# A two-layer decoder trunk: one norm of a token pair at a time, tokens loaded first, half of the first modulation sums on TensorE

## The chip, the cores and the metric

One core of a Trainium2 chip. The metric is the device time of one launch in microseconds, over several runs; a profiled execution of the same kernel gives the trace. A difference of 0.2% is about 3 us here.

## The reference

Sequence 512, width 1024, one batch, float32. Two layers: the first has dilated window attention (three groups of heads), the second has differential attention over keys and values that are computed once from the stream after layer 0. Each attention is followed by a gated convolutional feed-forward part. Every part is wrapped as below; the keys and values have a norm and a modulation of their own.

```python
c_act = jax.nn.silu(c)
for l in range(DEPTH):
    shift, scale, gate = ada_mod(c_act, mod_mix_w[l], mod_mix_b[l], 3)   # c_act @ w + b, split in 3
    if l == N_A_LAYERS:
        k_sh, v_sh = shared_kv(x, c_act, kv_norm, kv_mod_w, kv_mod_b, b_w_k, b_w_v, cos, sin)
    h = rms_norm(x, norm_pre_mix[l]) * (1.0 + scale) + shift
    y = mixer(h)                       # dilated (layer 0) or differential attention (layer 1)
    x = x + gate * rms_norm(y, norm_post_mix[l])
    shift, scale, gate = ada_mod(c_act, mod_ffn_w[l], mod_ffn_b[l], 3)
    h = rms_norm(x, norm_pre_ffn[l]) * (1.0 + scale) + shift
    x = x + gate * rms_norm(conv_ffn(h), norm_post_ffn[l])
```

## The kernel before

The program is written engine by engine, each with its own order of instructions, and semaphores between them (`wait_ge(*at.done(signal))`, `.then_inc(*at.here(signal))`). An engine executes its list in order, so a wait holds all that stands behind it. Weights come through a ring of three chunks (`raw`), are split into a high part by ScalarE (`split_head`, L1312) and a low part by VectorE (`split_rest`, L1815), and each product is three matmuls (high x high, high x low, low x high).

**The start.** SP's queue loads six small arrays of vectors (L453 to L456: c and the norm gains, 4 to 8 KB each), then x (L457, 2 MB), then eight tiles of 1 MB of the modulation matrix of layer 0 (`mstart`, L484) with the first value weights among them. ScalarE's queue loads thirteen small things: four lambda vectors, a gain, the positions (L1409 to L1411), and then seven tables of biases and convolution weights (L1412 to L1417). `mstart[:, j]` for j = 0, 1 is the upper and lower half of the rows for shift columns 0 to 511, j = 2, 3 the same for the scale, j = 4 to 7 the same for columns 512 to 1023. The product of c with these tiles is done by VectorE as a chain of multiply-adds (`start_chain`, L2039 and L2041, four instructions for each tile), in the order tiles 0 and 1, 2 and 3, and later 5, then 6 and 7; TensorE takes tile 4 (`shift_columns`, L758). TensorE then sums over the partitions by products with a column of ones (`start_sums`, L606), and VectorE reads the sums (`sums_read`) and makes the gain; only then can the normed and modulated h be made from the turned tokens `z0`, and the first product of TensorE with it begins (`values_chunk`, L777 and L793). Dummy matmuls (`keep_warm`, L578) stand in between. VectorE also computes the rotation angles (L2000 to L2010) before it reads the bias tables (L1976) and starts the chains; the angles go to ScalarE for the sines.

**A token stage** comes after each of the four parts. For four token tiles t: ScalarE sums the squares of y (`square_y`), GpSimd makes the reciprocal root, VectorE adds to x (`gained`, `added`), ScalarE sums the squares of the new x (`square_x`), and TensorE turns x times its root (`turn_x`, L674) into PSUM. Of a pair of tiles, ScalarE writes the front half of the normed columns into a buffer (`fronts`, L1367) and VectorE the back half (`backs`, L1876); ScalarE then makes the high parts (`heads`, L1376) and VectorE the low parts (`rests`, L1890), whose last instruction raises `n_ready`. After layer 0's feed-forward part there are two norms for each pair (`norms` has two entries: one for the shared keys and values, one for layer 1's queries), in the other stages one or none. After that stage TensorE runs `enter_b`: the products of the first value half (L1087) for token tiles 0 and 1, then 2 and 3. `V_BANKS` are the PSUM banks of these four tiles; the first pair is turned into banks 0 to 3, the second into banks 4 to 7.

## Time and profile before

| | |
|---|---|
| median of three runs | 1460.94 us (1459.55 to 1462.33) |
| the profiled execution's own time | 1459.9 us |
| its span, first to last instruction | 1458.0 us |
| TensorE matmul busy | 1407.2 us, 97% |
| VectorE busy | 889.1 us, 61% |
| ScalarE busy | 588.7 us, 40% |
| GpSimd busy | 146.2 us, 10% |
| mean granted TensorE clock | 0.986 |

A row of the timeline gives start, duration, engine, line, operation, output and inputs, count, and in brackets how long the engine had been idle and what ended the wait. PE is TensorE, DVE VectorE, ACT ScalarE, POOL GpSimd; SPq and ACTq are DMA issues. PEclk is the granted clock as a share of 2.4 GHz: 1.00 is 2.4 GHz and 0.50 is 1.2 GHz. A stretch ahead of the first record of the clock is shown as 1.00 whatever it was.

### The profile page before, as it was taken

The page shows a single profiled execution, that of the slowest core. Times are in us where ns is not written, and L with a number is a line of the kernel's source. Part 1 is how long each engine was busy: PE and PEld are TensorE (multiplying, and loading weights), DVE is VectorE, ACT ScalarE, POOL GpSimd, SP SyncE. Part 2 cuts the span into 40 slices and gives each one's busy share as a digit, 9 for nine tenths or more (in the row PEclk, how much of TensorE's full clock was granted, in tenths as well). Part 3 has the DMA queues.
Part 4 walks back from the last instruction along what each step waited for, and adds up shares of the span by engine and source line. Part 5 has one row for each costly group of instructions (what it writes and reads, how often), then busy time and mean ns, then how long its engine had stood idle before and what let it go on. Part 6 is the DMA issues. An engine that isn't in the chain of part 4 may idle for free.

```text
span 1458.0 us, 18234 instructions
## 1 busy us (share of the span) xinstructions
PE 1407.2 (97%) x7091; PEld 1153.7 (79%) x7096; DVE 889.1 (61%) x1572; ACT 588.7 (40%) x1018; POOL 146.2 (10%) x250
## 2 busy tenths in 40 slices
PE   4999999999999999999999999998999999999998
PEld 3789888888798788887887787776888878887886
DVE  7777877674458777763556538887358444443223
ACT  4533444345443334332124526776443333332212
POOL 2001100000211111110112101221221000000000
PEclk9999999999999999999999999998999999999999
DMA  9437423331146655552661221212126333232321
GB/s 334 140 85 233 145 88 117 101 102 30 29 137 199 185 169 178 179 182 87 202 188 58 87 73 58 59 59 87 30 85 186 92 96 92 88 100 89 100 89 70
DMA packets 168667, 171.51 MB, mean 118 GB/s; under 512 B 5269, under 2 KB 140806, under 8 KB 168582
## 3 DMA queue, kind: packets, MB, share of 16 engines
q1 hardware_dynamic: 154224, 119.59, 27.2%
q0 software_dynamic: 13824, 50.34, 10.7%
q8 instruction: 57, 0.93, 0.3%
q10 hardware_dynamic: 534, 0.41, 0.1%
q14 instruction: 28, 0.23, 0.0%
HBM read 168.22 MB, written 2.10 MB: 117 GB/s over the span
## 4 chain that ended last, share of the span: by engine, by line
PE 82%; DVE 8%; ACT 4%; issue 3%; POOL 2%; DMA 1%; SPq 0%; ACTq 0%; DVEq 0%; POOLq 0%
PE ps L624 19%; PE ps L552 15%; PE ps L554 15%; PE ps L553 15%; PE ps L1087 3%; PE ps L900 2%; PE ps L793 2%; PE ps L864 2%; ACT prob L1702 2%; PE ps L606 1%; PE ps L595 1%; PE ps L1204 1%; DVE prob L2355 1%; POOL osum L2537 1%; PE ps L674 1%
## 5 line engine op out<-in xcount | busy, mean ns | idle before, releaser
L552 PE MATMUL ps<-hhi,whi 128*128 128x512 f32 (+1 forms) x1008 | 398.6, 395 | 5.2 <-DVE hlo L1890 4.6
L1815 DVE TENSOR_TENSOR wlo<-raw,whi 128x1024 fp32r<-128x1024 f32 x200 | 244.0, 1221 | 245.7 <-ACT whi L1312 245.4
L554 PE MATMUL ps<-hhi,wlo 128*128 128x512 f32 (+1 forms) x1008 | 390.5, 387 | 0.0
L553 PE MATMUL ps<-hlo,whi 128*128 128x512 f32 (+1 forms) x1008 | 390.1, 387 | 0.0
L1312 ACT ACTIVATE whi<-raw 128x1024 fp32r<-128x1024 f32 x200 | 210.1, 1052 | 257.1 <-PE ps L624 175.7
L552 PEld LDWEIGHTS ps<-hhi,whi 128*128 128x128 f32 x1008 | 191.4, 190 | 47.0 <-issue 6.4
L554 PEld LDWEIGHTS ps<-hhi,wlo 128*128 128x128 f32 x1008 | 191.4, 190 | 41.9
L553 PEld LDWEIGHTS ps<-hlo,whi 128*128 128x128 f32 x1008 | 191.7, 190 | 39.6 <-issue 1.0
L1940 DVE SCALAR_TENSOR_TENSOR macc<-mraw,csil,macc 128x256 f32<-128x256 f32 x294 | 142.2, 484 | 13.4 <-DMA mraw<-in_mod_ffn_w_dram 4.2
L624 PE MATMUL ps<-whi,ghi 128*128 128x512 f32 x352 | 110.8, 396 | 1.7 <-DVE tmp L2294 1.7
L624 PE MATMUL ps<-whi,glo 128*128 128x512 f32 x352 | 110.8, 396 | 0.0
L624 PE MATMUL ps<-wlo,ghi 128*128 128x512 f32 x352 | 110.5, 394 | 0.0
L2278 DVE SCALAR_TENSOR_TENSOR tmp<-ps,convc,tmp 128x511 f32<-128x511 f32 x88 | 65.8, 748 | 51.5 <-ACT tmp L1640 50.0
L1650 ACT ACTIVATE ghi<-tmp 128x512 fp32r<-128x512 f32 x44 | 27.8, 632 | 155.5 <-DVE tmp L2294 155.5
L1640 ACT ACTIVATE tmp<-ps,convc 128x512 f32<-128x512 f32 x44 | 34.2, 778 | 114.6 <-PE ps L554 114.5
L624 PEld LDWEIGHTS ps<-whi,ghi 128*128 128x128 f32 x352 | 65.7, 188 | 18.7 <-DVE tmp L2294 2.6
L624 PEld LDWEIGHTS ps<-wlo,ghi 128*128 128x128 f32 x352 | 66.1, 188 | 16.1
L624 PEld LDWEIGHTS ps<-whi,glo 128*128 128x128 f32 x352 | 66.1, 188 | 15.9
L2500 POOL DMA_DIRECT2D mraw<-in_mod_ffn_w_dram x48 | 36.3, 756 | 352.3 <-DVE macc L1940 279.5
L2294 DVE TENSOR_TENSOR tmp<-ps,tmp 128x512 f32<-128x512 f32 x44 | 30.4, 690 | 58.5 <-issue 45.7
L2472 POOL TENSOR_SCALAR stat<-stat 128x1 f32<-128x1 f32 (+1 forms) x29 | 8.7, 301 | 471.8 <-ACT tmp L1351 426.3
L1647 ACT ACTIVATE tmp<-tmp 128x512 f32<-128x512 f32 x44 | 27.9, 633 | 50.6 <-DVE tmp L2278 50.6
(282 smaller groups left out, 2031.1 us busy)
## 6 DMA issues: line engine op xcount, KB each, us to landing
mraw<-in_mod_ffn_w_dram POOLq DMA_DIRECT2D x48, 512.0 KB, 4.2
raw<-in_ffn_w_gate_dram SPq DMA_DIRECT2D x44, 512.0 KB, 3.8
raw<-in_ffn_w_up_dram SPq DMA_DIRECT2D x44, 512.0 KB, 3.8
raw<-in_ffn_w_down_dram SPq DMA_DIRECT2D x44, 512.0 KB, 3.6
mraw<-in_mod_mix_w_dram POOLq DMA_DIRECT2D x32, 512.0 KB, 3.9
raw<-in_a_w_qkv_dram SPq DMA_DIRECT2D x28, 512.0 KB, 4.1
mstart<-in_mod_mix_w_dram SPq DMA_DIRECT2D x8, 1024.0 KB, 14.5
mraw<-in_kv_mod_w_dram POOLq DMA_DIRECT2D x16, 512.0 KB, 3.8
```

The source lines that it names most:

```text
L552: pe.matmul(out_, whi[:, slot, cols], rhs_hi, start=first, stop=False)
L553: pe.matmul(out_, whi[:, slot, cols], rhs_lo, start=False, stop=False)
L554: return pe.matmul(out_, wlo[:, slot, cols], rhs_hi, start=False, stop=last)
L624: mm = pe.matmul(ps[:, 2 * t + half, :], part[:, k, tile_cols(t)], w[:, half * 512:half * 512 + 512], start=(first and n == 0), stop=(last ...
L1087: mm = pe.matmul(ps[:, V_BANKS[t], :], a[:, k, tile_cols(t)], b[:, slot, w], start=(k == 0 and n == 0), stop=(k == DT - 1 and n == 2))
L1312: act.activation(whi[:, slot, :], raw[:, slot, :], ACT.Copy).then_inc(*at.here(hi_ready, ahead))
L1640: act.activation(tmp[:, 0, :], acc[at.at("bank", 3)], ACT.Identity, bias=convc[:, base + 3 * FT + ft:base + 3 * FT + ft + 1], scale=convc[ ...
L1815: dve.tensor_tensor(wlo[:, slot, :], raw[:, slot, :], head, ALU.subtract).then_inc(*at.here(lo_ready, ahead))
L1940: ins = dve.scalar_tensor_tensor(sum_, src, factor, sum_, ALU.mult, ALU.add)
L2278: ins = dve.scalar_tensor_tensor(conv, bank[:, 0:T - shift], tap(t, ft), conv, ALU.mult, ALU.add)
L2294: dve.tensor_tensor(tmp[:, 2, :], bank, tmp[:, 1, :], ALU.mult).then_inc(*at.here(acc_free))
L2500: pool.dma_start(mraw[:, at.at("mod", 2)], src).then_inc(*at.here(m_landed))
```

## The change

At the start: x is the first load on SP's queue; the six loads of vectors move to the head of ScalarE's queue, ahead of the lambdas and positions; the seven tables are issued after the two exponentials of ScalarE. VectorE reads the tables and runs its chains first, over tiles 0 and 2 (and later 5 and 7) alone; the angles come after them. TensorE multiplies tiles 1, 3, 4 and 6 with c in 16 one-column products each (`start_products`), accumulating in the same bank as the sums: tile 1 ahead of the turning of x, tile 3 between its sixth and seventh column tile, tiles 4 and 6 after the first value chunk. `WARM_SUMS` goes from 12 to 6, in two places. GpSimd makes the root of x ahead of the last mask.

In the stage with two norms: ScalarE and VectorE finish the first norm of a pair before they begin the second, with the splits of weight chunks between them. The second pair is turned into banks 0, 1, 5 and 6, after the value products of two chunks instead of one and after both halves of the second norm's buffer were written; the values of token tiles 0 and 1 go to banks 4 and 7. For one norm the order of instructions stays as it was.

```diff
-    WARM, WARM_START, WARM_SUMS = 24, 8, 12
+    WARM, WARM_START, WARM_SUMS = 24, 8, 6
...
-        V_BANKS = (2, 3, 4, 7)
+        V_BANKS = (4, 7, 2, 3)
+
+        def turned_banks(pair, norms):
+
+            return (0, 1, 5, 6) if pair and norms == 2 else range(4 * pair, 4 * pair + 4)
 
...
 
-            sp.dma_start(rows[C_ROW:C_ROW + DT, 0, :], c[0].rearrange("(r n) -> r n", n=P)).then_inc(*at.here(vec_landed))
-            for dst, src in ((PRE_MIX, norm_pre_mix), (POST_MIX, norm_post_mix), (PRE_FFN, norm_pre_ffn), (POST_FFN, norm_post_ffn)):
-                sp.dma_start(rows[dst:dst + 2 * DT, 0, :], src.rearrange("l (r n) -> (l r) n", n=P)).then_inc(*at.here(vec_landed))
-            sp.dma_start(rows[KVN:KVN + DT, 0, :], kv_norm.rearrange("(r n) -> r n", n=P)).then_inc(*at.here(vec_landed))
             sp.dma_start(x_tok[:], x[0].rearrange("(t p) d -> p t d", p=P)).then_inc(*at.here(x_landed))
...
 
-            def turn_x(t):
-
+            def turn_x(t, norms=1):
+
+                banks = turned_banks(t // 2, norms)
                 pe.wait_ge(*at.done(u_ready, t | 1))
                 pe.wait_ge(*at.done(x_rms, t))
                 for k in range(DT):
...
-                bank = job()
+            def start_columns(half):
+
+                return turned[at.at("tjob", 2)] if half else ps[:, 3, :]
+
+            def start_products(half, j):
+
+                pe.wait_ge(*at.done(c_ready))
                 pe.wait_ge(*at.done(mods_landed[j]))
+                if half and j == 4:
+                    job()
                 for n in range(4):
                     for k in range(DT // 2):
-                        ins = pe.matmul(bank[:, n:n + 1], mstart[:, j, k, tile_cols(n)], csil[:, k:k + 1],
-                                        start=(k == 0), stop=(k == DT // 2 - 1))
+                        row = j % 2 * (DT // 2) + k
+                        pe.matmul(start_columns(half)[:, j // 2 % 2 * 4 + n:j // 2 % 2 * 4 + n + 1], mstart[:, j, k, tile_cols(n)], csil[:, row:row + 1],
+                                  start=(j in (1, 4) and n == 0 and k == 0), stop=False, skip_group_check=True)
+
+            def start_sums(half):
+
+                pe.wait_ge(*at.done(m0_summed, 2 * half + 1))
+                for n in range(8):
+                    ins = pe.matmul(start_columns(half)[:, n:n + 1], macc0[:, n, :], onesf[:, 0:1], start=False, stop=True, skip_group_check=True)
                 job_done(ins)
...
 
+            start_products(0, 1)
             pe.wait_ge(*at.done(x_scaled, 1))
             pe.wait_ge(*at.done(x_scaled_too, 1))
             for k in range(DT):
+                if k == 6:
+                    start_products(0, 3)
                 if k < 4:
                     pe.wait_ge(*at.done(t_free, -1 - k % 2))
                 else:
@@ -816,12 +830,13 @@
                     ins = pe.transpose(ps[:, 4 + k % 4, tile_cols(t)], xn0[:, t, tile_cols(k)], identf[:])
...
             start_sums(0)
-            keep_warm(WARM_SUMS, ps[:, 3, :])
+            keep_warm(WARM_SUMS, ps[:, 2, :])
             values_chunk(0, 0)
-            shift_columns(4)
+            start_products(1, 4)
+            start_products(1, 6)
             values_chunk(0, 1, lambda: start_sums(1))
             keep_warm(WARM_START, ps[:, 4, :])
             values_chunk(0, 2)
@@ -1111,9 +1126,11 @@
                 for c in range(3):
                     pe.wait_ge(*at.done(lo_ready, c))
                     values_b(0, c, (0, 1))
-                    if c == 0:
-                        turn_x(2)
-                        turn_x(3)
+                    if c == 1:
+                        pe.wait_ge(*at.done(full_front, 1))
+                        pe.wait_ge(*at.done(full_back, 1))
+                        turn_x(2, 2)
+                        turn_x(3, 2)
...
-                    for n, norm in enumerate(norms):
-                        fronts(0, norm, n)
+                    fronts(0, norms[0])
                     heads(0, norms[0])
+                    if len(norms) > 1:
+                        split_next()
+                        fronts(0, norms[1])
                     square_x(3)
-                    for norm in norms[1:]:
-                        heads(0, norm)
                     split_next()
-                    split_next()
-                    for n, norm in enumerate(norms):
-                        fronts(1, norm, n)
+                    if len(norms) > 1:
+                        heads(0, norms[1])
+                    else:
+                        split_next()
                     for norm in norms:
+                        fronts(1, norm)
                         heads(1, norm)
...
+            act.dma_start(rows[C_ROW:C_ROW + DT, 0, :], c_rows).then_inc(*at.here(vec_landed))
+            for dst, src in ((PRE_MIX, norm_pre_mix), (POST_MIX, norm_post_mix), (PRE_FFN, norm_pre_ffn), (POST_FFN, norm_post_ffn)):
+                act.dma_start(rows[dst:dst + 2 * DT, 0, :], src.rearrange("l (r n) -> (l r) n", n=P)).then_inc(*at.here(vec_landed))
+            act.dma_start(rows[KVN:KVN + DT, 0, :], kv_norm.rearrange("(r n) -> r n", n=P)).then_inc(*at.here(vec_landed))
             for j, v in enumerate((b_lambda_q1, b_lambda_q2, b_lambda_k1, b_lambda_k2)):
                 act.dma_start(lamr[0:1, j, :], v).then_inc(*at.here(row_landed))
             act.dma_start(row1[0:1, 4, :], b_subln).then_inc(*at.here(row_landed))
             act.dma_start(posi[:], positions.to_broadcast([P, T])).then_inc(*at.here(row_landed))
+
+            act.wait_ge(*at.done(t_free))
+            act.activation(EXPC, vcol[:, C_ROW:C_ROW + DT], ACT.Exp, scale=-1.0).then_inc(*at.here(c_exped))
+            act.wait_ge(*at.done(lam_summed))
+            act.activation(lams[0:1, 2:4], lams[0:1, 0:2], ACT.Exp).then_inc(*at.here(lam_exped))
+            at.passed("tjob", 2)
             act.dma_start(rows[0:6 * DT, 1, :], mod_mix_b.rearrange("l (r n) -> (l r) n", n=P)).then_inc(*at.here(table_landed))
             act.dma_start(rows[6 * DT:12 * DT, 1, :], mod_ffn_b.rearrange("l (r n) -> (l r) n", n=P)).then_inc(*at.here(table_landed))
             act.dma_start(rows[12 * DT:14 * DT, 1, :], kv_mod_b.rearrange("(r n) -> r n", n=P)).then_inc(*at.here(table_landed))
             for layer in range(2):
                 act.dma_start(rows[0:3 * FT, 2 + layer, :], ffn_conv_w[layer].rearrange("w (r n) -> (w r) n", n=P)).then_inc(*at.here(table_landed))
                 act.dma_start(rows[3 * FT:4 * FT, 2 + layer, :], ffn_conv_b[layer].rearrange("(r n) -> r n", n=P)).then_inc(*at.here(table_landed))
-
-
-            act.wait_ge(*at.done(t_free))
-            act.activation(EXPC, vcol[:, C_ROW:C_ROW + DT], ACT.Exp, scale=-1.0).then_inc(*at.here(c_exped))
-            act.wait_ge(*at.done(lam_summed))
-            act.activation(lams[0:1, 2:4], lams[0:1, 0:2], ACT.Exp).then_inc(*at.here(lam_exped))
-            at.passed("tjob", 2)
 
...
-                    for n, norm in enumerate(norms):
-                        backs(0, norm, n)
-                    added(3)
+                    backs(0, norms[0])
+                    if len(norms) > 1:
+                        rests(0, norms[0])
+                        added(3)
+                        split_next()
+                        backs(0, norms[1])
+                        split_next()
+                        rests(0, norms[1])
+                    else:
+                        added(3)
+                        rests(0, norms[0])
+                        split_next()
+                        split_next()
                     for norm in norms:
-                        rests(0, norm)
-                    split_next()
-                    split_next()
-                    for n, norm in enumerate(norms):
-                        backs(1, norm, n)
-                    for norm in norms:
+                        backs(1, norm)
                         rests(1, norm)
...
 
+            bank = job_ready()
+            job_read(dve.tensor_copy(small[:, NEGLAM:NEGLAM + 1], bank[:, 0:1]))
+            for dst, n in ((bcol[:], NMOD), (convc[:, 0:CONV], CONV), (convc[:, CONV:2 * CONV], CONV)):
+                read_columns(dst, n)
+            dve.wait_ge(*at.done(t_free, -1))
+            dve.wait_ge(*at.done(t_free, -2))
...
+            def scale_last_tokens():
+
+                dve.wait_ge(*at.done(x_scale))
+                for t in (2, 3):
+                    dve.tensor_scalar(xn0[:, t, :], x_tok[:, t, :], X_RMS[:, t:t + 1], None, ALU.mult).then_inc(*at.here(x_scaled_too))
+                    at.passed("x_scaled_too")
+
+            def start_chain(j, dst, number):
+
+                sum_ = macc0[:, dst:dst + 4, :].rearrange("p a n -> p (a n)")
+                dve.wait_ge(*at.done(mods_landed[j]))
+                for k in range(DT // 2):
+                    src, row = mstart[:, j, k, :], j % 2 * (DT // 2) + k
+                    if k == 0:
+                        ins = dve.tensor_scalar(sum_, src, csil[:, row:row + 1], None, ALU.mult)
+                    else:
+                        ins = dve.scalar_tensor_tensor(sum_, src, csil[:, row:row + 1], sum_, ALU.mult, ALU.add)
+                    if k < DT // 2 - 1:
+                        chain(ins)
+                ins.then_inc(*at.here(m0_summed, number))
+
+            def sums_read(half):
+
+                bank = job_ready()
+                if not half:
+                    bank = ps[:, 3, :]
+                col, gain = MIX[0] + 4 * half, MIX[0] + DT + 4 * half
+                dve.tensor_tensor(modc[:, col:col + 4], bcol[:, col:col + 4], bank[:, 0:4], ALU.add)
+                job_read(dve.tensor_tensor(modc[:, gain:gain + 4], bank[:, 4:8], bcol[:, gain:gain + 4], ALU.add))
...
+
+            start_chain(0, 0, 0)
+            scale_last_tokens()
+            start_chain(2, 4, 1)
+            dve.wait_ge(*at.done(diffs_ready))
+            diffs = tmp[:, 3, 0:P].bitcast(I32)
+            chain(dve.tensor_single_scalar(diffs, diffs, 3, ALU.bitwise_and))
+            dve.tensor_scalar(near[:, P:2 * P], diffs, 0.0, MASKED, ALU.is_gt, ALU.mult).then_inc(*at.here(near_ready))
+
             a0, a1, k0 = ang[:, 0, :], ang[:, 1, :], ang[:, 2, :]
             two_pi = 2.0 * math.pi
...
-            start_chain((0, 1), 0, 0, scale_last_tokens)
-            start_chain((2, 3), 4, 1)
             split_rest(0)
             sums_read(0)
             h_rest(0, False)
             h_rest(1, True)
             split_rest(1)
-            start_chain((5,), 0, 2)
+            start_chain(5, 0, 2)
             h_rest(2, True)
             h_rest(3, True)
-            start_chain((6, 7), 4, 3)
+            start_chain(7, 4, 3)
             split_rest(2)
-            shift_read()
             sums_read(1)
...
+
+            pool.wait_ge(*at.done(x_squared, NT - 1))
+            rms(X_RMS, X_SUM, slice(0, NT)).then_inc(*at.here(x_scale))
+
+            pool.wait_ge(*at.done(near_ready))
+            select(near[:].rearrange("p (b k) -> p b k", k=P), [[0, 2], [-1, P]], 0, 1, MASKED).then_inc(*at.here(masks_ready))
 
             def token_stage(norms):
                 def of_y(t):
```

## Rows read from the trace of the kernel before

**Rows 1.** Timeline of TensorE, from the start to the first products.

```profile
6.70 2.29 PE L743 MATMUL ps<-onesf,row 1*128 1x1 f32 x10
...
12.97 0.45 PE L735 MATMUL ps<-identf,rows 112*128 112x112 f32 x1 [2.39 <-DMA rows<-in_ffn_conv_b_dram]
...
21.26 5.16 PE L816 MATMUL ps<-identf,xn 128*128 128x128 f32 x32 [3.69 <-ACT xn L1434]
...
31.23 3.54 PE L606 MATMUL ps<-onesf,macc 128*128 128x1 f32 x16 [2.22 <-issue]
...
38.64 0.59 PE L777 MATMUL ps<-whi,hhi 128*128 128x512 f32 x1
...
44.43 3.63 PE L758 MATMUL ps<-csil,mstart 128*128 128x1 f32 x32
...
52.35 1.84 PE L606 MATMUL ps<-onesf,macc 128*128 128x1 f32 x16
```

**Rows 2.** Waits of TensorE from 60 to 370 us: total, times, longest; the first.

```profile
PE ps L614 <- ACT probT L1526: 1.3, 1, 1.3
```

**Rows 3.** Windows of the start: each engine's busy time, PEclk, DMA share, GB/s.

```profile
21.00:24.00 3.00, 2.74 (x13) 2.74 (x14) 2.86 (x5) 1.40 (x3) 0.00 (x0) 1.00 1.05 385
...
31.00:38.00 7.00, 6.77 (x25) 4.63 (x26) 3.37 (x8) 2.73 (x4) 0.29 (x1) 0.51 1.05 387
...
48.00:52.00 4.00, 4.00 (x12) 3.14 (x12) 2.71 (x5) 0.00 (x0) 0.00 (x0) 0.57 0.02 6
```

**Rows 4.** Timeline of the DMA issues of SP and of ScalarE at the start.

```profile
3.38 0.40 SPq L457 DMA_DIRECT2D x_tok<-in_x_dram  x1
...
2.43 0.39 ACTq L1411 DMA_DIRECT2D posi<-in_positions_dram  x1
...
6.22 0.47 ACTq L1417 DMA_DIRECT2D rows<-in_ffn_conv_b_dram  x1
```

**Rows 5.** Timeline of VectorE at the start.

```profile
6.16 0.65 DVE L1972 TENSOR_TENSOR lamr<-lamr 1x128 f32<-1x128 f32 x1 [0.86 <-DMA posi<-in_positions_dram]
...
10.04 0.43 DVE L2000 CAST ang<-posi 128x512 f32<-128x512 int32 x1
...
17.89 0.49 DVE L2039 TENSOR_SCALAR macc<-mstart,csil 128x512 f32<-128x512 f32 x1
...
19.20 1.42 DVE L2028 TENSOR_SCALAR xn<-x_tok,stat 128x1024 f32<-128x1024 f32 x2
...
25.65 5.48 DVE L2041 SCALAR_TENSOR_TENSOR macc<-mstart,csil,macc 128x512 f32<-128x512 f32 x7
...
36.19 0.69 DVE L2075 TENSOR_TENSOR hlo<-tmp,hhi 128x512 fp32r<-128x512 f32 x1 [0.37 <-ACT hhi L1450]
```

**Rows 6.** Timeline of ScalarE at the start.

```profile
8.02 0.21 ACT L1421 ACTIVATE small<-vcol 128x8 f32<-128x8 f32 x1
...
12.50 1.06 ACT L1428 ACTIVATE tmp<-x_tok 128x1024 f32<-128x1024 f32 x1 [4.19 <-DMA x_tok<-in_x_dram]
```

**Rows 7.** Timeline of TensorE around the token stage with two norms.

```profile
794.42 5.13 PE L578 MATMUL ps<-causal,identb 128*128 128x512 bf16 x23
...
802.21 0.57 PE L1087 MATMUL ps<-whi,khi 128*128 128x512 f32 x1 [2.66 <-DVE klo L1890]
...
806.66 3.73 PE L674 MATMUL ps<-macc,x_tok 128*128 128x128 f32 x32
...
817.58 0.50 PE L1087 MATMUL ps<-whi,khi 128*128 128x512 f32 x1 [1.57 <-DVE klo L1890]
```

**Rows 8.** Timeline of ScalarE and VectorE in the same stage, first pair.

```profile
794.68 3.74 ACT L1367 ACTIVATE f_h<-ps,modc,presc 128x256 f32<-128x256 f32 x8
...
799.80 2.35 DVE L1890 TENSOR_TENSOR klo<-f_h,khi 128x1024 fp32r<-128x1024 f32 x2
```

**Rows 9.** Timeline of VectorE in a stage with one norm, second pair.

```profile
410.29 1.90 DVE L1876 TENSOR_SCALAR a_h<-ps,presc,modc 128x256 f32<-128x256 f32 x4 [6.20 <-PE ps L674]
...
413.35 2.36 DVE L1890 TENSOR_TENSOR hlo<-a_h,hhi 128x1024 fp32r<-128x1024 f32 x2 [1.15 <-ACT hhi L1376]
```

84 lines of the change are left out of this document (19 added, 65 removed).

## The prediction

> **What bounds the kernel now.** I read first the timeline of TensorE over the start [rows 1]: the reader is to see that its first real product (L777) comes at 38.64 us, and that from the sums at 31.23 on it hardly stops. Then its waits [rows 2]: from 60 to 370 us the longest is 1.3 us. So what the start loses or gains is not caught up later; I count it whole. Third the windows [rows 3], for the granted clock: about half (1.2 GHz) from 31 to 38 us and for most of 48 to 52, right behind the one-column products of L758. The first clock record lies later than the first products, so the shares shown ahead of it say nothing: the x turning had 13 matmuls in its first 3 us and the other 19 in the remaining 2.2 [rows 1, 3], which shows the lower level at first. The same matmul with one column costs 0.113 us at the upper level (32 in 3.63), 0.221 at the lower (16 in 3.54), and 0.229 at 6.70 us [rows 1].
>
> **Loads at the start.** x is issued at 0.7 instead of 3.38 us [rows 4], so it lands some 2.7 us earlier. Nothing needs that: ScalarE is still issuing. Its queue gets six vector loads ahead, so the positions, now sixth, become the twelfth issue: about 2.43 + 2.6 = 5.0 us (the six took SP until 3.38, from 0.7) [rows 4]. Before, the positions landed 3.7 us after their issue (2.43 to 6.16) [rows 4, 5], with little beside them; the last table took 6.75 us (6.22 to 12.97) [rows 1, 4], with x beside it. Now x is in front of all. So the positions land at P = 8.7 to 11.8; I take the middle, 10.3, as they meet x's first half. VectorE's vectors and both exponentials wait for them.
>
> By the Trainium skill, "DMA: Bandwidth & Descriptors", section "Issuing engines are not separate DMA queues", transfers started from different engines interleave on the same 16 DMA engines and a second issuer saves only issue time; that speaks against taking the vectors out of x's way like this. By it P is the upper end, and the sum would be about 1.5 us more; by the positions' own row about 1.6 less. The slow last table is the row that agrees.
>
> The seven tables are issued behind the exponentials, the first of which ended 8.23 - 6.16 = 2.1 us after the positions before, with ScalarE still busy with its issues; freed of these I take 1.4 [rows 5, 6]. Seven intervals between issues took 3.8 us (2.43 to 6.22) [rows 4], so the last table starts at about P + 4.8 and lands 3.7 to 6.75 later: T = P + 8.5 to P + 11.5, or 17.2 to 23.3, middle 20.3, against 12.97. Its readers follow: three transposes and reads, 1.2 us on TensorE and 1.6 on VectorE, my estimate from the 0.45 us transpose [rows 1].
>
> **VectorE.** Its first chain starts at T + 1.6 = 21.9 (before 17.89, with the angles between 10.04 and that in front) [rows 5]. A tile is four instructions of 0.49 to 0.78 us, 2.8 us; the scaling of the last tokens is 1.4 [rows 5]. So the scaling ends at T + 5.8 = 26.1 and the two chains at T + 8.6 = 28.9, where before they ended at 31.13. The angles behind them cost under 17.89 - 10.04 = 7.9 us, with a split of 1.2: VectorE is ready for the sums at 38 at the latest. ScalarE's path to the scaled tokens took 21.26 - 12.50 = 8.8 us from its first square [rows 1, 6]; from P + 1.4 + 3.8 = 15.5 that is 24.3. Neither ends last; TensorE does, as follows. GpSimd's reorder is worth a mask of under 1 us on this covered path, so nothing; x's wait hides it.
>
> **TensorE at the start.** Tile 1's products stand ahead of the turning of x, and behind the tables: they begin at T + 1.2 = 21.5. TensorE has done little before, so I price 32 matmuls at the lower level, 7.1 us: 28.6. The turning of x starts there instead of 21.26: +7.3. At the upper level they would take 3.6 and VectorE's 26.1 would decide. From the turning to the sums before: 31.23 - 21.26 = 10.0 us, the end of it waiting for VectorE. Now 5.2 for the turning, 3.6 to 7.1 for tile 3's products inside it (I take 4.6, nearer the upper level since 24 matmuls precede), and 2.1 for six dummies: 11.9, so +1.9. The sums cost 3.5 as before. After them h needed until 36.9, 2.1 us after the sums' end (34.77), and the dummies held the product until 38.64 [rows 1, 5]; six fewer give back the 1.7 us between. Sum so far: +7.3 + 1.9 - 1.7 = +7.5.
>
> Two dearer things follow. The first value products then come right behind one-column work and six dummies, partly at the lower level; up to 3.4 us of products there would cost half of that, I take +0.8 (0 to 1.7). And tile 6's products are 32 matmuls more between the two value chunks: 3.6 at the upper level, 7.1 at the lower. After the 3.6 us of L758 the clock fell [rows 1, 3], so the second such group falls into that; I take +5.0. What they replace on VectorE, 3.1 us of chain for tile 6, is not on the path: the sums at 52.35 came right behind a full TensorE. The start in all: 7.5 + 0.8 + 5.0 = +13.3.
>
> Bounds of the start. Low: T at 17.2 takes 3.1 off, and all one-column work at the upper level another 5.6 to 7.4 (2.5 where VectorE then decides, 1.0, 0.8, 1.4, and 1.7 in the sums); that leaves +2.8. High: T at 23.3 adds 3.0, and tile 3, the value products and tile 6 at their dear ends 2.5, 0.9 and 2.1: +21.8.
>
> **The stage with two norms.** Before, ScalarE and VectorE write both norms' halves of pair 0 (3.74 us), then split the first: n_ready comes at 802.15 and TensorE, whose dummies ended at 799.55, waits 2.66 us [rows 7, 8]. Now one norm's half, 1.9 us, leads: 794.68 + 1.9 + two high parts of 1.04 + the last low part of 1.2 = 800.0. The added tile 3, the splits and norm 2 come behind it. That is 2.1 us earlier and leaves no idle. The next 24 matmuls at 0.234 us (two chunks) bring TensorE to 805.6; the added wait for norm 2's halves ends, by adding VectorE's 1.2 (add), 1.2 (split) and 1.9, at 804.3, before that. The last root on GpSimd, behind square_x(3) at 802.8, has 4.6 us of room. The turning takes 3.6: 809.2. From turned to n_ready(2) one norm needs 415.7 - 410.3 = 5.4 us [rows 9]: 814.6, against 817.58. Gain 2.9, cut to 2.8 for hand-over. But the idle in front is then 2.7 us (812.0 to 814.7), as long as the 2.66 behind which this stage had the lower level; where it had 1.57 the clock stayed. That would cost 3.4 us at half speed, 1.6. I take -1.2, with 0 to -2.8 as bounds. Norm 2 ends by 819, used much later. The other token stages have one norm and the same order: nothing.
>
> **Sum.** +13.3 - 1.2 = +12.1 on the execution's own 1459.9: 1472.0. The median of the runs is 1.0 above that execution, inside their spread; I keep 1472.
>
> **The rivals.**
> *The start costs less, and slower all the same.* Small loads land as the positions did, T = 17.2: -3.1, so 1469; with the products between the levels, 1463 to 1469. For it: ScalarE's queue is its own. Against: the last table's 6.75 us.
> *The small loads are held behind x and the tiles.* T = 23.3 or later, with the clock low through tiles 4 and 6: 1475 to 1480.
> *Faster.* TensorE runs its one-column products at the upper level from tile 1 on. With T at 20.3 the turning then starts at 26.1 (+4.8), takes 3.7 + 3.6 with 1.3 of dummies (-1.4), the sums and h 1.8 + 2.1 where 7.4 stood (-3.5), tile 6 costs 3.6, and the value products after it save the 1.6 that they lose today: +1.9. With -2.8 in the norms, 1459; with T at 17.2, 1456. It decides where T is under about 19 as well. Against: 0.229 us in its first ten products and the fall behind L758.
> *The norms give nothing.* The turned tiles come late because the second norm's halves must be written before; then 1473. The 1.3 us of room speaks against it.
>
> **Chances.** Forecast with 1469 to 1475: 0.45. The cheaper start, 1463 to 1469: 0.25. Held loads, above 1475: 0.18. The upper level: 0.12, of which 0.07 faster by more than 0.2% (under 1458.0; 0.2% is about what a measurement tells from no change) and 0.05 within it. So slower 0.88. The norms that give nothing are 0.08 of the forecast's 0.45. The range 1460 to 1479 leaves out about 0.10 below (most of the upper-level case) and 0.06 above.
>
> **What would show it.** In the changed kernel: the last table's transpose (L735 there) at about 20 and not 13; the first group of one-column products at 0.22 us each, ending near 28.6; the first value product at about 46, and the two groups between the value chunks taking 8 to 11 us together. In the two-norm stage the first value product within 1 us of the last dummy, and the second wait between 2 and 3 us. I am wrong if the tables land near 15, if the one-column products run at 0.11 us from the start, or if TensorE's later waits shrink by what the start lost.

## The result, and the profile of the changed kernel

The changed kernel takes 1477.76 us (median; 1477.11 to 1481.8) against 1460.61 us for the kernel before (1459.55 to 1462.33): a ratio of 1.0128 [1.0115, 1.0141], 1.3% slower. The prediction said slower, 1472.0 us, with 1479 as the upper end. The median lies just under that end, and the ratio applied to the time before (1.0128 x 1460.61 = 1479.3) just over it. The direction was right; the loss is 17.2 us by the medians and 18.7 by the ratio, where 12.1 were forecast. The profiled execution took 1477.57 us with a span of 1475.8, so its trace can stand for the median.

TensorE at the start, the rows that answer to [rows 1]. The trace shows each float32 product with one column as two matmuls, so the 16 products of a tile stand as x32 and the 16 of the sums in the two-norm stage as x8 and x24:

```profile
8.12 0.37 PE L738 MATMUL ps<-identf,rows 80*128 80x80 f32 x1 [8.12 <-DMA rows<-in_kv_norm_dram]
12.38 2.26 PE L746 MATMUL ps<-onesf,row 1*128 1x1 f32 x10 [3.90 <-DMA posi<-in_positions_dram]
...
21.81 0.59 PE L738 MATMUL ps<-identf,rows 112*128 112x112 f32 x2 [5.58 <-DMA rows<-in_ffn_conv_b_dram]
...
22.82 6.89 PE L768 MATMUL ps<-csil,mstart 128*128 128x1 f32 x32
29.57 4.33 PE L830 MATMUL ps<-identf,xn 128*128 128x128 f32 x24
33.74 4.66 PE L768 MATMUL ps<-csil,mstart 128*128 128x1 f32 x32
38.26 1.95 PE L830 MATMUL ps<-identf,xn 128*128 128x128 f32 x8
40.00 2.77 PE L580 MATMUL ps<-causal,identb 128*128 128x512 bf16 x6
42.56 2.03 PE L775 MATMUL ps<-onesf,macc 128*128 128x1 f32 x16
...
46.84 0.47 PE L788 MATMUL ps<-whi,hhi 128*128 128x512 f32 x1 [0.94 <-DVE hlo L2069]
...
52.53 9.95 PE L768 MATMUL ps<-csil,mstart 128*128 128x1 f32 x64
...
73.40 0.58 PE L788 MATMUL ps<-whi,hhi 128*128 128x512 f32 x1
```

The last row is the first product of value chunk 2. In the kernel before it is this row:

```profile
58.50 0.58 PE L777 MATMUL ps<-whi,hhi 128*128 128x512 f32 x1
```

So by here the change has lost 14.9 us: 8.2 in front of the first value product (46.84 against 38.64), and 6.7 behind it. The one long wait ahead of the new work is the one at 21.81, for the tables. VectorE read the positions late too:

```profile
12.31 0.28 DVE L1999 TENSOR_TENSOR lamr<-lamr 1x128 f32<-1x128 f32 x1 [6.23 <-DMA posi<-in_positions_dram]
```

ScalarE's issues and its first exponential show where both delays come from:

```profile
5.07 0.36 ACTq L1434 DMA_DIRECT2D posi<-in_positions_dram  x1
...
13.08 0.21 ACT L1437 ACTIVATE small<-vcol 128x8 f32<-128x8 f32 x1 [6.34 <-DVE vcol L2003]
13.09 0.34 ACTq L1441 DMA_DIRECT2D rows<-in_mod_mix_b_dram  x1
...
15.63 0.37 ACTq L1446 DMA_DIRECT2D rows<-in_ffn_conv_b_dram  x1
```

The positions took 7.2 us from issue to landing (5.07 to 12.31) where they took 3.7 before [rows 4, 5], and only after the exponential at 13.08 do the seven tables go out. In the windows the reader is to see PEclk and PE's count of instructions:

```profile
core 0: us, PE busy (x) PEld busy (x) DVE busy (x) ACT busy (x) POOL busy (x), PEclk, DMA share, GB/s
56.60:66.80 10.20, 10.20 (x40) 9.23 (x40) 0.78 (x1) 0.00 (x0) 0.00 (x0) 0.50 0.18 53
...
831.00:834.50 3.50, 3.50 (x11) 2.76 (x10) 3.50 (x5) 2.90 (x3) 0.00 (x0) 0.56 0.02 5
845.00:848.00 3.00, 3.00 (x26) 2.82 (x24) 0.43 (x1) 1.73 (x3) 0.00 (x0) 1.00 0.21 81
848.50:855.30 6.80, 6.80 (x18) 4.35 (x18) 0.47 (x2) 1.19 (x2) 0.00 (x0) 0.50 0.23 77
```

TensorE is busy in all of these windows; what falls is its clock, to the level of 1.2 GHz. The first covers the second half of the 64 one-column products and the value products behind them; before, the lower level lasted 3.4 us there [rows 3]. The last one has no counterpart in the kernel before. Over the whole span the mean granted clock is 0.981 against 0.986 before: 28.0 us lost to the clock against 20.4 (estimates from span times missing share), so about 7.6 of the 17.8 us between the spans, to 1 us for the rounding. The stretch ahead of the first record of the clock counts as full speed in both.

The stage with two norms, where [rows 7] are the rows of before:

```profile
809.28 5.34 PE L580 MATMUL ps<-causal,identb 128*128 128x512 bf16 x24
815.20 0.50 PE L1102 MATMUL ps<-whi,khi 128*128 128x512 f32 x1 [0.58 <-DVE klo L1912]
...
830.14 0.49 PE L1102 MATMUL ps<-whi,khi 128*128 128x512 f32 x1 [2.69 <-DVE klo L1912]
...
846.60 3.55 PE L608 MATMUL ps<-onesf,macc_late 128*128 128x1 f32 x24
```

The one-column sums behind it, in the kernel before:

```profile
831.68 0.95 PE L606 MATMUL ps<-onesf,macc 128*128 128x1 f32 x8
832.49 2.82 PE L606 MATMUL ps<-onesf,macc_late 128*128 128x1 f32 x24
```

From the last dummy's end to the second restart it takes 830.14 - 814.62 = 15.5 us, against 817.58 - 799.55 = 18.0 before: 2.5 us gained. The offset to the kernel before goes from +15.1 ahead of the stage to +12.6 at the restart, +14.1 behind the lower clock at 831 (where the sums begin), and +17.4 behind the one at 848.5. It ends at +17.8, the difference of the spans (1475.8 - 1458.0).

### The profile page after: what moved, and what is told of

The parts are those of the page before. It is cut to its first block, busy times and chain, and to the rows that moved or that the text cites. A ratio compares the mean times of both kernels' runs of the same rounds, so it can differ in the third digit from the quotient of the medians.

```text
span 1475.8 us, 18393 instructions
## 1 busy us (share of the span) xinstructions
PE 1426.2 (97%) x7180; PEld 1173.2 (79%) x7180; DVE 880.7 (60%) x1559; ACT 589.5 (40%) x1018; POOL 143.4 (10%) x250
## 3 DMA queue, kind: packets, MB, share of 16 engines
q0 software_dynamic: 13824, 50.34, 10.5%
## 4 chain that ended last, share of the span: by engine, by line
PE 82%; DVE 7%; ACT 4%; issue 2%; POOL 2%; DMA 2%; ACTq 0%; DVEq 0%
PE ps L626 19%; PE ps L554 15%; PE ps L556 14%; PE ps L555 14%; PE ps L1102 3%; PE ps L915 2%; PE ps L804 2%; PE ps L879 2%; ACT prob L1724 2%; PE ps L768 1%; PE ps L597 1%; PE ps L1221 1%; PE ps L608 1%; PE ps L677 1%; DVE prob L2373 1%
## 5 line engine op out<-in xcount | busy, mean ns | idle before, releaser
L626 PEld LDWEIGHTS ps<-whi,ghi 128*128 128x128 f32 x352 | 65.7, 188 | 18.4 <-DVE tmp L2312 2.5
L626 PEld LDWEIGHTS ps<-whi,glo 128*128 128x128 f32 x352 | 66.1, 188 | 16.4
L2312 DVE TENSOR_TENSOR tmp<-ps,tmp 128x512 f32<-128x512 f32 x44 | 30.4, 690 | 58.7 <-issue 45.5
L2128 DVE TENSOR_TENSOR tmp<-ps,cosT 128x512 f32<-128x512 f32 x40 | 27.5, 689 | 36.4 <-PE ps L556 36.4
```

The lines of the kernel that those rows point to most:

```text
L626: mm = pe.matmul(ps[:, 2 * t + half, :], part[:, k, tile_cols(t)], w[:, half * 512:half * 512 + 512], start=(first and n == 0), stop=(last ...
L2312: dve.tensor_tensor(tmp[:, 2, :], bank, tmp[:, 1, :], ALU.mult).then_inc(*at.here(acc_free))
```

## The experiments

Ten kernels ran, on three chips; each is compared with runs of the kernel before on its own chip (medians 1460.1, 1460.5 and 1459.54 us). The chips thus differ by 1 us, and the intervals of the ratios are wider, 1.4 to 3.1 us to either side: a difference between the medians of two variants of the changed kernel is not good to better than 2 to 3 us. Where a trace shows it too, its figure stands beside it.

**The two halves of the change, each alone.** First, the two-norm stage put into the kernel before (with the new order in `token_stage` on ScalarE and VectorE), with the start left as it was.

```diff
-        V_BANKS = (2, 3, 4, 7)
+        V_BANKS = (4, 7, 2, 3)
...
-                    if c == 0:
-                        turn_x(2)
-                        turn_x(3)
+                    if c == 1:
+                        pe.wait_ge(*at.done(full_front, 1))
+                        pe.wait_ge(*at.done(full_back, 1))
+                        turn_x(2, 2)
+                        turn_x(3, 2)
```

> The kernel before with the order of the two-norm stage alone (banks, order of the norms, the turning behind two value chunks). Theory (the loss is made at the start): 1 to 2.5 us faster than before, 1458 to 1460; the wait ahead of the first value products under 1 us, n_ready of the second pair about 2.5 us earlier, of which 1.6 may go to a stretch of the lower clock behind the remaining wait. Rival (the changed stage brings the clock down later, as in the 6.8 us at half clock behind its one-column sums in the changed kernel): slower than before by 1 to 3 us.

Measured: 1459.84 us, ratio 1.0000 [0.9988, 1.0013]. The trace has the forecast wait and the fall behind it:

```profile
811.90 0.57 PE L1092 MATMUL ps<-whi,khi 128*128 128x512 f32 x1 [2.71 <-DVE klo L1899]
```

```profile
812.20:815.60 3.40, 3.40 (x9) 2.63 (x8) 3.40 (x6) 2.97 (x4) 0.00 (x0) 0.50 0.00 0
```

The reordered norms neither gain nor lose what can be measured; the 1 to 2.5 us expected did not show. The interval is 1.8 us to either side, so a net gain of about 1 us is not excluded.

Second, the start alone, without any of the two-norm stage.

```diff
+            start_products(0, 1)
             pe.wait_ge(*at.done(x_scaled, 1))
...
+                if k == 6:
+                    start_products(0, 3)
...
-            shift_columns(4)
+            start_products(1, 4)
+            start_products(1, 6)
```

> The kernel before with the changes of the start alone (loads, products of tiles 1, 3 and 6 on TensorE, order of VectorE and GpSimd, six dummies fewer in two places). Theory: 14 to 15 us slower than before, 1474 to 1476. Rival (the stage and the clock behind it make 3 to 5 us of the 17): then the same 14 to 15 us here, but the first run is slower than before; if the start alone gives 17 or more, the stage is innocent.

Measured: 1476.09 us, ratio 1.0116 [1.0102, 1.0130]: 16.0 us slower by the medians, more than the 14 to 15 expected. Chunk 2 starts at 72.86, 14.4 us late. So the kernel with the start alone has the whole loss but some 1.7 us. This kernel too has a stretch at the lower level behind the one-column sums of the two-norm stage (850.6 to 854.0, PEclk 0.51), though that stage is unchanged in it; at half speed it is worth 1.7 us.

**The loads.** The changed kernel with the loads of before: the six vectors on SP's queue ahead of x, the tables ahead of the exponentials.

```diff
+            sp.dma_start(rows[C_ROW:C_ROW + DT, 0, :], c[0].rearrange("(r n) -> r n", n=P)).then_inc(*at.here(vec_landed))
...
             sp.dma_start(x_tok[:], x[0].rearrange("(t p) d -> p t d", p=P)).then_inc(*at.here(x_landed))
...
-            act.dma_start(rows[C_ROW:C_ROW + DT, 0, :], c_rows).then_inc(*at.here(vec_landed))
...
+            act.dma_start(rows[0:6 * DT, 1, :], mod_mix_b.rearrange("l (r n) -> (l r) n", n=P)).then_inc(*at.here(table_landed))
...
             act.wait_ge(*at.done(t_free))
             act.activation(EXPC, vcol[:, C_ROW:C_ROW + DT], ACT.Exp, scale=-1.0).then_inc(*at.here(c_exped))
```

> The changed kernel with the loads in the order of before (vectors on SP's queue, tables ahead of the exponentials, x after the vectors). Theory (the late tables hold TensorE's first products and these the turning of x): the tables land at 13 us again, but tile 1 only at 18, its products end at 25 and the turning starts there instead of 29.6: 4 to 5 us faster than the changed kernel, about 1473. Rival (x and the tiles 2.6 us earlier were worth something, the tables are covered): no change or slower than the changed kernel.

Measured: 1472.5 us, ratio 1.0090 [1.0076, 1.0104], 5.3 us less than the changed kernel. First value product 41.62, chunk 2 at 68.18. The tables no longer hold tile 1 here, but its own load does:

```profile
18.12 6.96 PE L770 MATMUL ps<-csil,mstart 128*128 128x1 f32 x32 [3.92 <-DMA mstart<-in_mod_mix_w_dram]
```

The reverse is the kernel before with only the new order of loads, the same lines with the signs turned.

> The kernel before with the order of the loads of the change alone (x first, vectors on ScalarE's queue, tables behind the exponentials). Theory (the positions land at 12.3 and the tables at 21.8 us, as in the changed kernel, and VectorE does angles, then tables, then its chains): chains start at 24 instead of 17.9, sums at 37 instead of 31.2: 6 us slower than before, about 1466. Rival (only the products on TensorE cost; the loads are covered): within 1.5 us of before.

Measured: 1464.85 us, ratio 1.0033 [1.0019, 1.0047], +4.4 where about 6 were expected.

```profile
21.93 0.45 PE L733 MATMUL ps<-identf,rows 112*128 112x112 f32 x1 [5.71 <-DMA rows<-in_ffn_conv_b_dram]
...
36.87 1.97 PE L604 MATMUL ps<-onesf,macc 128*128 128x1 f32 x16 [1.31 <-issue]
...
42.72 0.58 PE L775 MATMUL ps<-whi,hhi 128*128 128x512 f32 x1
```

The tables land 9 us late (21.93 against 12.97), and the first value product 4.1 us late. Between the two, VectorE's angles fill the wait for the tables (15.7 to 22.0 us) instead of standing in front of the chains, and the sums ran at the upper level this time (1.97 us against 3.54 in [rows 1]). The loads cost about the same without the other edits (4.4) and with them (5.3), and the interval of the first lies above 1: they are a cause of their own.

Which part of the new load order? The changed kernel with one thing different, the seven tables issued ahead of the two exponentials:

```diff
-            act.wait_ge(*at.done(t_free))
-            act.activation(EXPC, vcol[:, C_ROW:C_ROW + DT], ACT.Exp, scale=-1.0).then_inc(*at.here(c_exped))
-            act.wait_ge(*at.done(lam_summed))
-            act.activation(lams[0:1, 2:4], lams[0:1, 0:2], ACT.Exp).then_inc(*at.here(lam_exped))
...
             act.dma_start(rows[0:6 * DT, 1, :], mod_mix_b.rearrange("l (r n) -> (l r) n", n=P)).then_inc(*at.here(table_landed))
...
+            act.wait_ge(*at.done(t_free))
+            act.activation(EXPC, vcol[:, C_ROW:C_ROW + DT], ACT.Exp, scale=-1.0).then_inc(*at.here(c_exped))
+            act.wait_ge(*at.done(lam_summed))
+            act.activation(lams[0:1, 2:4], lams[0:1, 0:2], ACT.Exp).then_inc(*at.here(lam_exped))
```

> The changed kernel with the seven tables issued ahead of the exponentials, everything else as changed. Theory (the first products wait for the tables alone): tables land at 15 to 17 us, products of tile 1 end near 24 and the turning starts there instead of 29.6: 4 to 5.5 us faster than the changed kernel, about 1473. Rival (the exponentials and the squares behind the seven issues are late instead, or the positions land later): less than 2 us faster.

Measured: 1471.93 us, ratio 1.0073 [1.0052, 1.0094], 5.8 us less.

```profile
12.57 2.26 PE L746 MATMUL ps<-onesf,row 1*128 1x1 f32 x10 [4.08 <-DMA posi<-in_positions_dram]
...
16.35 1.22 PE L738 MATMUL ps<-identf,rows 112*128 112x112 f32 x3
17.36 6.89 PE L768 MATMUL ps<-csil,mstart 128*128 128x1 f32 x32
...
41.37 0.47 PE L788 MATMUL ps<-whi,hhi 128*128 128x512 f32 x1 [0.94 <-DVE hlo L2069]
```

The table transposes at 16.35 no longer wait for a load, and chunk 2 starts at 67.91, 5.5 us earlier. The positions still land at 12.5. So what the loads cost comes from issuing the tables behind an exponential that waits for the positions. The time is that of the loads of before (1472.5), so the vectors moved to ScalarE's queue cost nothing that can be measured here once the tables go first. With the loads of before the products of tile 1 had to wait for their own tile until 18.12, and here they start at 17.36; where nothing waits for that tile the comparison could come out otherwise.

**Tile 6.** The changed kernel with tile 6 back in VectorE's chain with tile 7:

```diff
             start_products(1, 4)
-            start_products(1, 6)
             values_chunk(0, 1, lambda: start_sums(1))
...
-            start_chain(7, 4, 3)
+            start_chain(6, 4, 3, (7,))
```

> The changed kernel with tile 6 summed by VectorE again, so 32 one-column matmuls between the value chunks instead of 64. Theory (TensorE sets the end there and the second 32 run at the lower clock): 5 to 6.5 us faster than the changed kernel, 1471 to 1473; the 32 take 3.6 us. Rival (VectorE's chain of tiles 6 and 7 ends too late): the sums wait for VectorE and the gain is under 3 us.

Measured: 1469.4 us, ratio 1.0057 [1.0037, 1.0077], 8.4 us less, more than the 5 to 6.5 expected.

```profile
52.03 3.85 PE L768 MATMUL ps<-csil,mstart 128*128 128x1 f32 x32
...
66.11 0.59 PE L788 MATMUL ps<-whi,hhi 128*128 128x512 f32 x1
```

```profile
55.30:58.70 3.40, 3.40 (x11) 2.82 (x11) 3.26 (x5) 0.69 (x1) 0.00 (x0) 0.50 0.00 0
58.70:67.00 8.30, 8.23 (x44) 6.31 (x45) 5.96 (x13) 3.88 (x5) 0.00 (x0) 1.00 0.22 65
```

Chunk 2 starts 7.3 us earlier (66.11 against 73.40), of which 0.5 stand ahead of the products (52.03 against 52.53). The lower level lasts 3.4 us, and the clock is up again at 58.7, where the changed kernel stays down until 66.8. Tile 6 thus costs its own products and three times the stretch at 1.2 GHz. Most of that stretch falls on its own products: the group of 64 takes 9.8 us to the next product and the group of 32 takes 3.7, which is 6.1 us for the second 32; the twelve value products behind take 4.9 us against 4.2.

**The second fall in the two-norm stage.** In the changed kernel the 16 one-column sums, 32 matmuls, stand in a row at 845.8, and the clock falls while they run, at 848.4. Here 8 sums come (16 matmuls), then half of the key product (12 full matmuls), then the other 8:

```diff
-                columns_of([macc[:, j, :] for j in range(4)] + [macc_late[:, j, :] for j in range(2 * PAIRS_LATE - 4)])
+                sums = [macc[:, j, :] for j in range(4)] + [macc_late[:, j, :] for j in range(2 * PAIRS_LATE - 4)]
+                bank = job()
+                for j, sum_ in enumerate(sums):
+                    if j == len(sums) // 2:
+                        part_of_b(1, 0)
+                    ins = pe.matmul(bank[:, j:j + 1], sum_, onesf[:, 0:1], start=True, stop=True)
+                job_done(ins)
...
-                part_of_b(1, 0)
                 part_of_b(1, 1)
```

> The changed kernel with the 16 one-column sums ahead of the second value half of layer 1 (L608, 32 matmuls in one piece) cut in two, with half of a key product between the two pieces. Theory (these sums in one piece bring the clock down for 6.8 us, which costs 3.3 us where a window of the clock falls on them): no fall of the clock at 848 to 855 us, 2 to 3.5 us faster than the changed kernel in the executions that have it, 1.5 to 3 us in the median. Rival (the fall comes from the wait at 827 to 830 us and follows it by itself): the fall stays, no change.

Measured: 1473.56 us, ratio 1.0092 [1.0075, 1.0109], 4.2 us less.

```profile
845.85 1.03 PE L1148 MATMUL ps<-onesf,macc_late 128*128 128x1 f32 x8
...
849.63 1.84 PE L1148 MATMUL ps<-onesf,macc_late 128*128 128x1 f32 x16
```

```profile
848.50:855.30 6.80, 6.80 (x36) 5.22 (x35) 0.17 (x1) 1.20 (x2) 0.00 (x0) 1.00 0.23 77
```

In the same 6.8 us TensorE now does 36 matmuls instead of 18, at the upper level. From the first of the sums to the end of the key product the trace is 3.3 us shorter (845.04 to 855.93 against 845.79 to 859.98). The median is 4.2 us less, above the 1.5 to 3 expected; the trace was 0.8 us ahead before it came to the sums, which the edit doesn't touch.

**Do the three causes add?** The changed kernel with the three edits together: tables early, tile 6 back, sums eight and eight.

> The changed kernel with three edits: the seven tables issued ahead of the two exponentials (worth 5.8 us by itself), tile 6 back on VectorE (8.4 us by itself) and the 16 one-column sums of the two-norm stage taken eight and eight with half a key product between (4.2 us by itself). What is left of the change: the early vectors, tiles 1 and 3 on TensorE at the start, and the new order of the two norms. Theory (three separate causes, which add): 1477.8 - 5.8 - 8.4 - 4.2 = 1459.4, the time before within 0.2%; in the trace the first value product at about 41.4 and chunk 2 at 67.9 - 7.2 = 60.7, and no fall of the clock near 845. Rival A (the causes overlap, since each of them moves where the clock falls): 1463 to 1466, with chunk 2 beyond 62 or a new stretch at the lower level somewhere behind 66 us. Rival B (tiles 1 and 3 on TensorE are a cost of their own, hidden so far by the late loads): the turning of x stays near 24 against 21.3 and the time is 1462 to 1463.

Measured: 1460.9 us against 1459.54 before, ratio 1.0016 [1.0004, 1.0028]. Singly they gave back 5.8 + 8.4 + 4.2 = 18.4 us, together 16.9 by the medians. By the ratios it is 23.7 against 16.4, with the noise of five measurements in it, by my estimate some 6 us from their intervals. The starts in the traces are the sharper test: 5.5 and 7.3 us singly, 12.7 together (73.40 to 60.73).

```profile
17.32 6.89 PE L768 MATMUL ps<-csil,mstart 128*128 128x1 f32 x32
24.07 5.36 PE L830 MATMUL ps<-identf,xn 128*128 128x128 f32 x24
...
40.99 0.48 PE L788 MATMUL ps<-whi,hhi 128*128 128x512 f32 x1 [0.94 <-DVE hlo L2074]
...
60.73 0.58 PE L788 MATMUL ps<-whi,hhi 128*128 128x512 f32 x1
```

Chunk 2 is at 60.73, as expected to 0.1 us, and still 2.2 us behind the kernel before: that is rival B of this run in part. The turning starts at 24.07 instead of 21.26, so tile 1 on TensorE, ahead of it, costs a little of its own. The time that remains, 0.6 to 4.1 us by the interval, fits these 2.2.

**Can products on TensorE ever pay here?** The kernel before with one edit: tile 0 (not 1) goes to TensorE, into its idle time between the tables and the turning of x; the tables keep their early loads, VectorE's chains run over tiles 1, 2 and 3, and the dummies become 2 and 6.

```diff
+                for n in range(4):
+                    for k in range(DT // 2):
+                        pe.matmul(ps[:, 3, n:n + 1], mstart[:, 0, k, tile_cols(n)], csil[:, k:k + 1],
+                                  start=(n == 0 and k == 0), stop=False, skip_group_check=True)
...
+            tile_products()
             pe.wait_ge(*at.done(x_scaled, 1))
...
-            keep_warm(WARM_SUMS, ps[:, 3, :])
+            keep_warm(2, ps[:, 2, :])
             pe.wait_ge(*at.done(z_out, DT - 1))
             start_sums(0)
-            keep_warm(WARM_SUMS, ps[:, 3, :])
+            keep_warm(6, ps[:, 2, :])
...
-            start_chain((0, 1), 0, 0, scale_last_tokens)
+            start_chain((1,), 0, 0)
+            scale_last_tokens()
```

> The kernel before (its loads, its token stages) with tile 0 of the modulation in 16 one-column products on TensorE in the idle time ahead of the turning, VectorE's chains over tiles 1, 2 and 3 only, and 2 and 6 dummies around the sums. Theory (there the one-column products are free, as TensorE is idle from 17.6 to 21.3 us and VectorE sets the end): products from 15.3 to 22.4, sums at 28.5 instead of 31.2, first value product at 34 to 35.5 instead of 38.6: 2 to 4 us faster than before. Rival (fewer dummies leave the clock low for the value products, and the turning is 1 us later): within 1 us of before.

Measured: 1458.55 us, ratio 0.9981 [0.9970, 0.9992].

```profile
17.15 0.59 PE L735 MATMUL ps<-identf,rows 88*128 88x88 f32 x2 [3.63 <-DVE small L2033]
17.53 6.89 PE L768 MATMUL ps<-csil,mstart 128*128 128x1 f32 x32
24.29 5.22 PE L831 MATMUL ps<-identf,xn 128*128 128x128 f32 x32
...
35.54 0.77 PE L791 MATMUL ps<-whi,hhi 128*128 128x512 f32 x1 [0.73 <-DVE hlo L2092]
...
43.75 3.63 PE L758 MATMUL ps<-csil,mstart 128*128 128x1 f32 x32
...
57.81 0.59 PE L791 MATMUL ps<-whi,hhi 128*128 128x512 f32 x1
```

The idle time was smaller than it looks: the products are queued behind the table transposes, which wait 3.6 us for VectorE's angles, so the turning of x slips by 3.0 us. The first value product comes 3.1 us earlier all the same, since VectorE's chains no longer hold the sums and fewer dummies stand behind them. But the 24 value products then take 8.2 us (35.54 to 43.75), where they took 5.8 in the kernel before: the clock is at the lower level until 41.0. So at chunk 2 (57.81 against 58.50) only 0.7 us are left. This is what the run's rival said, in part. The fewer dummies are not apart from the tile in this run: in the kernel before they held the first value product from 36.9 to 38.64, so 1.7 of the 3.1 us could be theirs, and a kernel with only that edit was not run. One tile in idle time, with fewer dummies, is a small gain; a tile in a full stretch is a loss of 7.

**The best of it together.** Tile 0 in idle time, the two-norm stage of the change, and the sums eight and eight.

> The kernel before with everything that helped alone: tile 0's 32 one-column products in TensorE's idle time at the start (1.9 to 2.8 us by itself), the two-norm stage of the change (0 by itself: 2.5 us at the wait, 1.6 back to the lower clock), and the 16 one-column sums there taken eight and eight. Theory (the gains add, and the split sums keep the clock up behind them): 1460.5 - 2.4 - 0 to 1 = 1457 to 1458, ratio 0.998, no stretch at the lower level at 845. Rival (a start that is earlier moves the phase of the clock's falls, and one of them takes the gain back): 1459.5 to 1461, with the trace showing one more stretch at half clock than the tile 0 kernel has.

Measured: 1454.93 us against 1459.54 before, ratio 0.9975 [0.9965, 0.9984]: faster than both kernels. The 0.998 expected lies in the interval; the medians differ by 4.6 us where 2.5 to 3.5 were expected. The clock held at the sums:

```profile
826.00:835.00 9.00, 9.00 (x54) 7.33 (x53) 1.40 (x2) 2.35 (x4) 0.00 (x0) 1.00 0.26 89
```

```profile
56.15 0.58 PE L796 MATMUL ps<-whi,hhi 128*128 128x512 f32 x1
...
811.16 0.54 PE L1107 MATMUL ps<-whi,khi 128*128 128x512 f32 x1 [2.71 <-DVE klo L1919]
```

Chunk 2 starts at 56.15, 1.7 us earlier than with tile 0 alone (57.81), though nothing in front of it differs between the two, and their first value products start at 35.55 and 35.54. The stretch at the lower level lies otherwise: here it ends at 36.6 and the 24 products take 6.2 us, there it lasts until 41.0. The second wait of the norms is 2.71 us again. How much of the gain over tile 0 alone belongs to the norms, to the sums and to that shift was not separated.

## Why the prediction was right in its direction and wrong in its size

The direction, the place and the mechanism of the start held: the start carries most of the loss, TensorE ends last there, one-column products run at the lower level, and nothing behind catches it up (the offset is +14.9 at chunk 2 and +15.1 ahead of the two-norm stage; between 272 and 334 us of the changed kernel it is only +13.4, as the kernel before has a stretch at the lower level at 201 us that the changed one has at 335). The size was wrong: +12.1 forecast, +17.8 between the spans. Two steps failed. What lies behind the first value products of the two-norm stage was put at nothing, and there the clock fell once more, for 3.3 us. And tile 6 was priced at 5.0 us and took 6.8. The rest is smaller errors that partly cancel. By the prediction's steps:

- **P and T.** Forecast 10.3 and 20.3, measured 12.31 and 21.81. P lies above the upper end of 11.8. The page "DMA: Bandwidth & Descriptors" of the Trainium skill (section "Issuing engines are not separate DMA queues") says that transfers started by different engines interleave on the same 16 DMA engines; by it the prediction had P at the upper end, and the trace sides with that: 7.2 us for the positions instead of 3.7. My middle was wrong, and so was reading the row of before as likely for a small load that starts in the middle of x. T was late by only 1.5: the last table was issued at 15.63, which is P + 3.3 instead of P + 4.8, and landed 6.2 us later, where the middle had 5.2.
- **Tile 1 and the turning of x.** Forecast 7.1 us at the lower level from T + 1.2, ending at 28.6; measured 6.89 us from T + 1.0, ending at 29.7. The shift of 1.0 against the forecast is T's 1.5 less what these two saved. The start of the turning moved by 8.3 us against 7.3.
- **From the turning to the sums.** Forecast 11.9, measured 42.56 - 29.57 = 13.0; tile 3's 4.66 us was right (4.6), the six dummies took 2.6 at the lower level instead of 2.1, and the turning itself 5.9 (4.2 and 1.7) instead of 5.2. The sums took 2.03 where I had kept 3.5, which gave 1.5 back. First value product +8.2 against +7.5: right to 1 us, but by errors of +1.0, +1.1 and -1.5 that cancel, so partly by luck.
- **The first value products at the lower level, +0.8.** Not there: the 24 of them take 5.7 us (46.84 to 52.53), 0.24 us each, as in the kernel before (5.8).
- **Tile 6, +5.0.** The mechanism was right, the size was not. Against the kernel before, the group of one-column products grew from 3.5 to 9.8 us and the twelve value products behind it took 4.9 instead of 4.4: 6.8 us in all, and 6.8 also against the kernel with tile 6 back on VectorE; the median says 8.4. I had priced the second group of 32 at a mixed clock (bounds 3.6 to 7.1); it ran almost wholly at the lower level, which lasted 10.2 us here against 3.4 with one group. The upper bound held in the trace, so the fault is the middle.
- **The start in all.** Forecast +13.3, measured +14.9 at chunk 2: 1.6 us short. Inside that sum the value products (-0.9) and the sums (-1.5) offset the turning (+1.0), the way from it to the sums (+1.1) and tile 6 (+1.8).
- **The stage with two norms, -1.2.** The steps came as written: the first value product 0.6 us behind the last dummy, the second wait 2.69 us (forecast 2.7), 2.5 us gained (forecast 2.8), and the lower clock behind it. The offset moves by -1.0 over the stage. By itself the stage measures 1.0000, which holds -1.2. GpSimd's last root, 817.6 to 819.2, was early enough.
- **What had no term.** The fall at 848.5 behind the one-column sums, +3.3 us in the trace, 4.2 in the median. I costed what lies behind the two-norm stage at nothing, because its instructions stay as they are; but the clock under them changed. The 5.7 us between the forecast +12.1 and the spans' +17.8 are then 3.3 here, 1.6 in the start, 0.2 in the norms (-1.0 against -1.2), and drifts of 0.2 between 73 and 800 us and 0.4 behind 855.
- **The range.** The prediction's own upper bound for the start, +21.8, would have reached 1481.7 with nothing gained in the norms; the stated end of 1479 left that out, at a chance of 0.06.
- **The rivals.** "Held loads" had the time right (1475 to 1480). Its T of 23.3 was half true, and its low clock through tiles 4 and 6 was true for all but the first 4 us of them; but 3.3 us of the loss lie behind 848, where it had none, so its time is partly luck. "Cheaper start" fell with T at 21.8 and not 17.2, "upper level" at 0.215 us for each one-column matmul of tile 1. The last one's idea, that one-column products cost little, did not hold in a full stretch; in idle time it was tried only together with fewer dummies. "The norms give nothing" had the mechanism wrong (the turning at 820.90 did not wait, and the second wait ended 2.5 us earlier), and its outcome can't be told from the forecast: by itself the stage gave nothing that can be measured.

What stays open: why the clock falls at the one-column sums of the two-norm stage in some kernels and not in others. Of the nine kernels that have these sums in one piece, six fall there: the changed kernel and those with the loads back, tile 6 back or tables early for 6.8 us, the start alone and tile 0 in idle time for 3.4. Three do not: the kernel before, the norms alone and the loads alone, whose 32 matmuls take 3.5 us. The kernel with tile 0 in idle time has the two-norm stage of the kernel before, so the fall is no property of the changed stage. The three kernels with split sums have no fall. There is one trace of each kernel, so how often each falls isn't known; only the splitting was tried.

## What to carry to other kernels

A matmul with one column is no cheap matmul: on a full TensorE it costs its own 0.11 to 0.22 us and, after a long row of them, half the clock of the rest of the row and of the real products behind. So price a second group behind a first at the lower level (6.3 us for 32 here, not 3.6), and the products behind with it; in this kernel breaking the row up with full matmuls kept the clock up. A load that is issued behind an instruction that waits for another load pays both landings one after the other; ask of each moved load what its issuing engine waits for first. And a stage whose instructions don't change can still change its time: look in both traces at the granted clock behind each row of one-column matmuls, and widen the range by a few microseconds for such a place.

## What the runs showed of the hardware

- A row of 64 one-column matmuls with TensorE 100% busy came with 10.2 us at 1.2 GHz (granted clock 0.50, 56.6 to 66.8); a row of 32 at the same place with 3.4 us. All five traces with 64 show the 10.2 and all seven with 32 the 3.4. The lower level came while the engine had no idle time.
- 16 + 12 full + 16 matmuls instead of 32 in a row went with the clock at 2.4 GHz (36 matmuls in 6.8 us instead of 18), in three kernels of three; 32 in a row did so in three of nine.
- The runs of one kernel spread over 1.6 us (loads back, four runs) to 10.5 us (loads alone, ten runs), and over 7.5 with the norms alone, more than any of the norm's terms. Kernels with the same start differ at chunk 2 in their traces: by 1.7 us for the two with tile 0 in idle time, by 1.6 for the kernel before and the norms alone (58.50, 56.87). A single trace is thus no measure of a term of 1 to 2 us.
- The 256 KB of positions took 7.2 us to land where x (2 MB) was issued 4.3 us ahead of them on another queue and tiles of 1 MB behind it, and 3.7 us where they were issued 1 us ahead of x.
